# Block 1's attention in a one-core transformer kernel: from probabilities stationary, token rows out, to values stationary in two column halves, feature rows out

## The reference, cut to what matters

```python
s = einsum('bqkgd,bskd->bkgqs', q, k) * ATTN_SCALE
p = softmax(s, axis=-1)
a = einsum('bkgqs,bskd->bqkgd', p, v)
...
mix = concatenate([rmsnorm(a, attn_out_norm), rmsnorm(sc, conv_out_norm)], axis=-1)
x = x + m[:, :, 5] * (mix @ w_mix_out)
```

## Time and profile before

| | us |
|---|---|
| median of 3 runs | 1551.4 (1549.38 to 1552.7) |
| the profiled execution, its own time | 1551.04 |
| its span in the profile | 1548.8 |
| PE busy | 1414.5 (91%) |
| DVE busy | 1071.8 (69%) |
| ACT busy | 598.5 (39%) |
| attention stage (first scores to first `out` c matmul) | 439.7 to 501.6 |

### The profile page before, as it was taken

The page is one execution under the profiler, slowest core; times in us unless marked ns, Lnnn a source line. Parts: engine busy times, 40 slices in busy tenths (PEclk is TensorE's granted clock), DMA queues, the critical chain, the costliest instruction groups (busy, mean ns, idle before and its releaser), DMA issues.

```text
span 1548.8 us, 20067 instructions
## 1 busy us (share of the span) xinstructions
PE 1414.5 (91%) x7471; PEld 1053.9 (68%) x7471; DVE 1071.8 (69%) x2243; ACT 598.5 (39%) x1349; POOL 383.4 (25%) x377
## 2 busy tenths in 40 slices
PE   8999999999999999999999988999988777778777
PEld 6788888889887999999899955665433323223222
DVE  4787775547876687777896476757798666666454
ACT  4422122224556544445565233423343333333222
POOL 0100110002100100011006134445555444445330
PEclk7999999999999999999999999999999999999999
DMA  8864685446641465555545699999999999999997
GB/s 332 294 219 129 202 290 175 140 138 184 214 139 54 128 206 184 171 172 182 153 148 190 229 383 414 419 421 421 421 421 421 421 422 421 421 421 421 422 421 293
DMA packets 86479, 435.96 MB, mean 281 GB/s; under 512 B 9520, under 2 KB 13616, under 8 KB 53616
## 3 DMA queue, kind: packets, MB, share of 16 engines
q0 software_dynamic: 45024, 298.08, 48.2%
q1 hardware_dynamic: 41360, 136.62, 27.1%
HBM read 433.61 MB, written 1.05 MB: 281 GB/s over the span
## 4 chain that ended last, share of the span: by engine, by line
PE 61%; DMA 21%; DVE 13%; ACT 3%; issue 1%; POOL 0%; SPq 0%; ACTq 0%; POOLq 0%
PE ps L623 14%; PE ps L625 14%; PE ps L624 14%; DMA ring<-in_puv,AB 13%; PE ps L1064 10%; DMA HF<-in_puv,AB 7%; PE ps L984 5%; DVE WR L1454 2%; DVE ring L2242 1%; ACT WR L1084 1%; PE ps L663 1%; DMA ring<-in_f1i 1%; DVE HF L2242 1%; PE ps L1003 0%; DVE AF L2242 0%
## 5 line engine op out<-in xcount | busy, mean ns | idle before, releaser
L623 PE MATMUL ps<-HR,WR 128*128 128x512 f32 (+2 forms) x1064 | 344.8, 324 | 3.3 <-DVE WR L1454 1.4
L625 PE MATMUL ps<-HR,WR 128*128 128x512 f32 (+2 forms) x1064 | 339.7, 319 | 0.0
L624 PE MATMUL ps<-HR,WR 128*128 128x512 f32 (+2 forms) x1064 | 339.6, 319 | 0.0
L1454 DVE TENSOR_TENSOR WR<-ring,WR 128x1024 fp32r<-128x1024 f32 (+1 forms) x217 | 252.8, 1172 | 114.6 <-ACT WR L1084 114.4
L1084 ACT CAST WR<-ring 128x1024 fp32r<-128x1024 f32 (+1 forms) x217 | 212.6, 986 | 277.1 <-PE ps L625 273.5
L623 PEld LDWEIGHTS ps<-HR,WR 128*128 128x128 f32 x1064 | 202.7, 191 | 20.3 <-issue 2.4
L625 PEld LDWEIGHTS ps<-HR,WR 128*128 128x128 f32 x1064 | 202.6, 190 | 13.9
L624 PEld LDWEIGHTS ps<-HR,WR 128*128 128x128 f32 x1064 | 202.8, 191 | 13.7 <-issue 0.2
L1064 PE MATMUL ps<-AF,AB 128*128 128x512 f32 x264 | 126.9, 604 | 34.5 <-ACT AB L1439 34.5
L1429 ACT ACTIVATE AB<-AB 128x2 f32<-128x2 f32 x129 | 26.2, 203 | 322.0 <-DVE AB L2242 321.9
L623 PE MATMUL ps<-AR,WR 128*128 128x256 f32 (+1 forms) x471 | 147.4, 313 | 2.4 <-DVE AF L1835 2.4
(11 more groups left out here) (339 smaller groups left out, 2340.6 us busy)
## 6 DMA issues: line engine op xcount, KB each, us to landing
AB<-in_w_adaT POOLq DMA_DIRECT2D x56, 512.0 KB, 4.8
ring<-in_f1i SPq DMA_DIRECT2D x44, 512.0 KB, 4.8
ring<-in_f2i SPq DMA_DIRECT2D x44, 512.0 KB, 3.7
ring<-in_w SPq DMA_DIRECT2D x29, 512.0 KB, 3.7
ring<-in_f1o SPq DMA_DIRECT2D x21, 512.0 KB, 4.2
ring<-in_w_ada SPq DMA_DIRECT2D x16, 512.0 KB, 7.6
ring<-in_f2o SPq DMA_DIRECT2D x16, 512.0 KB, 3.7
ring<-in_mi SPq DMA_DIRECT2D x12, 512.0 KB, 4.5
```

Source lines behind the costliest of these rows:

```text
L623: e.matmul(o, l[0], r[0], start=first, stop=False)
L624: e.matmul(o, l[0], r[1], start=False, stop=False)
L625: return e.matmul(o, l[1], r[0], start=False, stop=last)
L1454: e.tensor_tensor(WS[:, m % NSP, 1, 0:nk * cols], ring[:, ring_of(m) % NS, 0:nk * cols], WS[:, m % NSP, 0, 0:nk * cols].bitcast(F32), ALU. ...
```

## The change

The product with the values is turned round. `pv` is now a step for two heads, one of each key/value head: the values (128 keys by 64 features) are stationary and the transposed exponentials move, 128 columns. The even head's result goes to partitions 0 to 63 and column half 0 of the array, the odd head's to partitions 64 to 127 and column half 1. The output has features on the partitions, so it needs no transpose, but the softmax sums and the norm, which were one number per partition, now are one number per column:

- `an` i 0: DVE takes the reciprocal of the sums, ACT copies it over 64 columns each into `aN` (128x512), PE transposes that ("over", 4 transposes). p 1: ACT copies it from PSUM to `R(2, 4)`.
- p 2: DVE multiplies `o` with it. p 3: ACT squares. p 4: PE sums the squares over partitions with ones (4 matmuls, line 831), DVE makes the reciprocal, 128x128. p 5 (`roots` for tile 0): ACT root, 128x128, and DVE applies root and gain in four instructions of 128 columns. p 6: ACT and DVE make high and low part from SBUF.
- The gain comes as four columns of the constants, so one broadcast DMA (`aon`) goes.

```diff
+    norms[8] = [("an", 0, 0)]
+    norms[9].append(("an", 0, 1))
-             12: [("an", 0, 0)], 13: [("an", 0, 1)], 15: [("roots",)], 16: [("cn", 2, 0)], 17: [("cn", 2, 1), ("cn", 2, 2)],
-             18: [("cn", 2, 3)], 19: [("cn", 2, 4), ("an", 0, 2)]}
+             12: [("an", 0, 2), ("an", 0, 3)], 13: [("an", 0, 4)], 15: [("roots",)], 16: [("cn", 2, 0), ("an", 1, 0)],
+             17: [("cn", 2, 1), ("cn", 2, 2), ("an", 1, 1)], 18: [("cn", 2, 3)], 19: [("cn", 2, 4), ("an", 0, 5)]}
-        if n >= 4:
-            out.append(("pv", n - 4))
+        if n >= 4 and n % 2:
+            out.append(("pv", (n - 5) // 2))
-    out += [("an", 1, 0), ("an", 1, 1), ("an", 1, 2), ("out", "c", 0), ("an", 0, 3), ("out", "c", 1), ("an", 1, 3),
-            ("out", "c", 2), ("out", "c", 3)]
+    out += [("an", 1, 2), ("an", 1, 3), ("out", "c", 0), ("an", 0, 6), ("an", 1, 4), ("out", "c", 1), ("an", 1, 5),
+            ("out", "c", 2), ("an", 1, 6), ("out", "c", 3)]
...
                     for k in range(4):
-                        x = e.matmul(o, PT[:, s[1] % 4, k, :], kvN[:, k, 128 + 64 * (hd % 2):192 + 64 * (hd % 2)],
-                                     start=k == 0, stop=k == 3)
-                    x.then_inc(*mm.to("pv", s[1]))
+                        for g in range(2):
+                            x = e.matmul(o[64 * g:64 * g + 64, :], kvN[:, k, 128 + 64 * g:192 + 64 * g],
+                                         PT[:, (2 * s[1] + g) % 4, k, :], start=k == 0, stop=k == 3)
+                            if k == 3:
+                                x.then_inc(*mm.to("pv", 2 * s[1] + g))
...
+                elif s[0] == "an" and s[2] == 4:
+                    o = bank("rms", "a", s[1])[:, 0:128]
+                    q.wait_ge(*ac.at("sq", "a", s[1]))
+                    for j in range(4):
+                        x = e.matmul(o, K("ones"), R(2, 4)[:, 128 * j:128 * j + 128], start=j == 0, stop=j == 3)
...
+                    if p == 0:
+                        q.wait_ge(*dv.at("over sums", i))
+                        e.copy(aN[:, i, :].rearrange("p (h d) -> p h d", h=8),
+                               hs[:, 104 + 8 * i:112 + 8 * i].unsqueeze(2).broadcast_to([128, 8, 64])).then_inc(
+                                   *ac.to("spread sums", i))
+                    elif p == 1:
+                        evac(R(2, 4), ("over", i), bank_of("over", i)[:, :])
...
+                    elif p == 4:
+                        recip(("a", i), ra_[:, i, :], 128, 1.0 / 512)
...
-                    e.dma_start(aon, T["aon"].partition_broadcast(128)).then_inc(s_aon, 16)
```

More of the change, by code:

```diff
@@ L399, in program @@
         cq, sq_, ck_, sk_ = (AB[:, 2048 + 128 * n:2176 + 128 * n].rearrange("p (i d) -> p i d", i=2) for n in range(4))
-        aon = AB[:, 2560:3072]
+        ra_ = AB[:, 2560:2816].rearrange("p (i q) -> p i q", i=2)
         gqk = K("gqk").rearrange("p (n d) -> p n d", n=4)
@@ L814, in tensor_program @@
                 elif s[0] == "an" and s[2] == 0:
[L815 to L818, removed]
+                    o = bank("over", s[1])
+                    q.wait_ge(*ac.at("spread sums", s[1]))
                     for j in range(4):
                         x = e.transpose(o[:, 128 * j:128 * j + 128], aN[:, s[1], 128 * j:128 * j + 128], K("ident"))
-                    x.then_inc(*mm.to("turn", "a", s[1]))
+                    x.then_inc(*mm.to("over", s[1]))
+                elif s[0] == "an" and s[2] == 2:
+                    banks.held.discard(banks.of["o", s[1]])
+                elif s[0] == "an" and s[2] == 4:
[3 more added lines that the diff above has]
+                        x = e.matmul(o, K("ones"), R(2, 4)[:, 128 * j:128 * j + 128], start=j == 0, stop=j == 3)
+                    x.then_inc(*mm.to("rms", "a", s[1]))
                 elif s[0] == "out":
@@ L1241, in scalar_program @@
                     root(("c",), R(0, 1))
-                    root(("a", 0), hs[:, 122:123])
+                    root(("a", 0), ra_[:, 0, :])
                 elif s[0] == "cn" and s[1] == 2 and s[2] < 4:
@@ L1246, in scalar_program @@
                     e.copy(MX[k][0], F[:, k % 3, 0:256]).then_inc(*ac.to("mx hi", k))
[L1247 to L1258, removed]
+                elif s[0] == "an":
+                    _, i, p = s
+                    if p == 0:
[5 more added lines that the diff above has]
+                        evac(R(2, 4), ("over", i), bank_of("over", i)[:, :])
+                    elif p == 3:
+                        q.wait_ge(*dv.at("ps", "o", i))
+                        e.activation(R(2, 4), aN[:, i, :], ACT.Square).then_inc(*ac.to("sq", "a", i))
+                    elif p == 5 and i:
+                        root(("a", 1), ra_[:, 1, :])
+                    elif p == 6:
+                        q.wait_ge(*dv.at("an", i))
+                        e.copy(MXR[:, 0, 4:8, 128 * i:128 * i + 128], aN[:, i, :].rearrange("p (j q) -> p j q", j=4)).then_inc(
+                            *ac.to("mxa hi", i))
                 elif s[0] == "out":
@@ L1828, in vector_program @@
                     _, i, p = s
-                    ri, ra_ = hs[:, 104 + 8 * i:112 + 8 * i], hs[:, 122 + i:123 + i]
                     if p == 0:
                         q.wait_ge(*ac.at("ps", "s", 8 * i + 7))
-                        e.reciprocal(ri, hs[:, 88 + 8 * i:96 + 8 * i]).then_inc(*dv.to("rsum", i))
-                        q.wait_ge(*dv.now())
+                        e.reciprocal(hs[:, 104 + 8 * i:112 + 8 * i], hs[:, 88 + 8 * i:96 + 8 * i]).then_inc(*dv.to("over sums", i))
+                    elif p == 2:
@@ L1834, in vector_program @@
                         q.wait_ge(*mm.at("pv", 8 * i + 7))
[L1835 to L1844, removed]
-                        q.wait_ge(*ac.at("root", "a", i))
[L1846 to L1849, removed]
+                        q.wait_ge(*ac.at("over", i))
@@ new lines, in vector_program @@
+                        e.tensor_tensor(aN[:, i, :], bank_of("o", i)[:, :], R(2, 4), ALU.mult).then_inc(*dv.to("ps", "o", i))
+                    elif p == 4:
+                        recip(("a", i), ra_[:, i, :], 128, 1.0 / 512)
+                    elif p == 5:
+                        q.wait_ge(*ac.at("root", "a", i))
+                        for j in range(4):
+                            a = aN[:, i, 128 * j:128 * j + 128]
+                            e.scalar_tensor_tensor(out=a, in0=a, scalar=C("aon")[:, j:j + 1], in1=ra_[:, i, :], op0=ALU.mult,
+                                                   op1=ALU.mult).then_inc(*dv.to("an", i))
+                    elif p == 6:
@@ L1850, in vector_program @@
                         hi, low = (MXR[:, n, 4:8, 128 * i:128 * i + 128] for n in range(2))
                         q.wait_ge(*ac.at("mxa hi", i))
-                        e.tensor_tensor(low, bank_of("turn", "a", i)[:, :].rearrange("p (j q) -> p j q", j=4),
-                                        hi.bitcast(F32), ALU.subtract).then_inc(*dv.to("ps", "turn", "a", i))
-                        dv.also("mxa", i)
+                        e.tensor_tensor(low, aN[:, i, :].rearrange("p (j q) -> p j q", j=4), hi.bitcast(F32),
+                                        ALU.subtract).then_inc(*dv.to("mxa", i))
@@ L2507, in layout @@
         "conv": cw, "con": cols(i["conv_out_norm"][0]),
+        "aon": cols(i["attn_out_norm"][0][heads]),
         "kvn": cols(i["kv_norm_g_2"][0]), "qn2": cols(i["q_norm_g_2"][0]), "kn2": cols(i["k_norm_g_2"][0]),
@@ L2520, in layout @@
         "miq": wide(mi[:, heads], 512), "mikv": wide(mi[:, 512:768], 256), "mi": tiles(mi[:, 768:]),
-        "moc": pairs(mo[512:]), "moa": pairs(mo[:512][heads]), "aon": i["attn_out_norm"][0][heads],
+        "moc": pairs(mo[512:]), "moa": pairs(mo[:512][heads]),
         "f2i": tiles(i["w_ffn2_in"][0]), "f2o": tiles(i["w_ffn2_out"][0]),
```

13 lines of the change are left out of this document (7 added, 6 removed).

## The result

Before 1552.37 us (median of 17 runs, 1549.38 to 1560.67), after 1557.46 (17 runs, 1553.49 to 1562.1). Ratio 1.0033, 95% interval 1.0024 to 1.0042: slower by 0.33%, some 5.1 us. The forecast was 1555.5 and slower.

The account below looks back on a forecast made before the run. PE, busy 91% of the span, was taken to pass its time on nearly one for one. Walk terms -1.0 + 2.65 - 0.6 + 3.0 - 1.35 + 0.2 = +2.9, clock +1.4, total +4.3: 1555.5 us, range 1552.3 to 1559.

Parts of the forecast that it names:

- The walk: Attention stage followed in after's order with before's durations, between pairs of `front`, through the `out` tiles: +2.9 us without clock.
- the clock: Falls to 1.2 GHz behind PE waits: one of two new waits costs 1.5, the old fall keeps its price: +1.4 us.
- the pair: Two heads' `pv` product on column halves takes 1.15 us instead of 1.64, saving 0.5.
- Rival (b): A `pv` pair costs less, 0.82 us (total 1553.7) or 0.5 (1551.9), so not slower; chance 0.12.
- Rival (c): The column halves do not overlap: pair 2.1 us, +5.7 more, total 1561.2; chance 0.08.
- the first and third wait: PE idles ahead of "over": 2.85 us for tile 0, behind DVE's late reciprocal, and some 4.6 for tile 1.
- No wait before the first `out`: Before's 2.43 us PE wait for the bank of `o` goes, as `out` has another bank.
- the second wait: PE idles 2.75 us before the sum over partitions (line 831), ahead of `front` 14, waiting for ACT's square.
- the sentence that no PSUM bank handed out again is still in use: Said of the part up to `front` 8: no reused bank makes PE wait; that part changes by -1.0 us.
- Rival (a): The clock stays up behind both new waits: +2.9 us, 1554.4, just inside no change; chance 0.22.

Follow-up runs that it names:

- x1: After with throwaway matmuls filling PE's three long waits: 1552.24 us, ratio to before 1.0000.
- x7: Before with five throwaway matmuls filling PE's 2.43 us wait ahead of the first output tile: 1549.46 us, ratio to before 0.9980.
- x4: After with tile 0's reciprocal and copy of sums ahead of the last filler's weight, PE's transposes behind the third pair: 1553.22 us, ratio to before 1.0009.
- x2: After with the bank of `o` of tile 0 given back one step later, so `back` 11 takes another: 1557.28 us, ratio to before 1.0027.
- x3: After with a pair's two column halves one after the other instead of alternating: 1559.4 us, ratio to before 1.0044.
- x10: After with five throwaway matmuls in the first of the three long waits only: 1555.03 us, ratio to before 1.0020.
- x8: Before with the bank of `o` of tile 1 held until the first output tile has another: 1547.18 us, ratio to before 0.9964.
- x5: After reordered: x4 and x2 together, tile 0's sum of squares and tile 1's copy and transposes also moved: 1545.84 us, ratio to before 0.9954.
- x9: x5 with a pair's two column halves one after the other instead of alternating: 1547.48 us, ratio to before 0.9967.

## Why the prediction was right, and where it was off

**Right: slower, by waits.** x1 runs after's order at full clock, x7 before's. Their stretches are 91.25 and 88.21, difference 3.04; by the ratios 3.1. The walk's sum without the clock was +2.9. Part of this closeness is luck: behind `front` 12 the walk is 0.4 too low for one part and 0.3 too high for the next.

| part | walk | x1 | after |
|---|---|---|---|
| to `front` 8, against before | -1.0 | -1.16 | -1.16 |
| `front` 8 to 10 | 9.35 | 9.29 | 11.11 |
| `front` 10 to 12 | 4.1 | 4.17 | 5.19 |
| `front` 12 to 14 | 6.8 | 7.21 | 9.47 |
| `front` 14 to the first `out` | 11.3 | 10.98 | 12.82 |

**Right: the pair.** 1.02 us and 0.1 for the entry, 1.12 for the forecast 1.15. Rival (b), 0.82, is out. The Trainium skill, page TensorEngine Tiling (Array Packing), section Theoretical Speedup, puts the gain for a dimension of 64 or less at up to 2x; here 1.64 to 1.12 is 1.46x. Rival (c) is out; its 2.1 was wrong as a bound too, since the halves in turn cost 1.51. Why a 128-column matmul beside another half is cheaper than `total`'s column is open.

**Right: the first and third wait.** 2.74 for 2.85 and 4.22 for 4.6, with the releasers named, the reciprocal behind the weight's low part (478.97 behind 477.83). x4 undid exactly that. No wait before the first `out`.

**Wrong place: the second wait.** The prediction had it before 831, released by 1269, with `back` 11 and the pair ahead of it. It stood at `back` 11, released by DVE's product (1852), which ends at 492.70 + 0.69 = 493.39; `back` 11 starts at 493.44. The step that failed is the sentence that no PSUM bank handed out again is still in use. I made it for the part up to `front` 8, where it holds, and did not ask again after `("an", 0, 2)`, where `Banks.take` gives `back` 11 the bank that this same step is emptying. Size 2.80 for 2.75, but `back` 11 and the pair moved behind it: 7.21 in x1 for 6.8. x2 put the wait where I had it, at 2.64, and the part took 6.91.

**Mis-sized: the clock.** The term was +1.4, for one new fall of two possible, with the old one taken over at its 1.5. It was a choice, not a reading. After had three falls in the profiled execution, and without them it is 5.2 us faster (x1). Before without its fall is 3.1 us faster (x7), though only 1.5 of it shows in the profiled execution. So by the times the clock adds 5.2 - 3.1 = 2.1 to the difference and the waits the other 3.1. That the two make up the measured 5.1 to 5.2 is no check, since the same four kernels give both; and each ratio's interval is 1.3 to 1.6 us either way, so the times alone can't tell 2.1 from 1.4. By the stretches of the profiled executions the clock adds (97.84 - 91.25) - (89.71 - 88.21) = 5.09 and the waits 3.04. What is shown is three falls where the forecast had two, and waits of some 3 us by both rulers; the clock's share in an average execution lies somewhere about 2 and stays rough. That the total came so near, 5.1 for 4.3, owes something to luck.

The miss in absolute time is 1557.5 for 1555.5. Half of it is the median of before, 1552.4 over 17 runs for 1551.4 over 3, 0.8 is the difference (5.1 for 4.3), and 0.2 is the prediction's own sum: 1551.4 and 4.3 make 1555.7.

Rival (a), no fall behind the new waits, is out for the profiled execution by its stretches of 0.50 and 0.54. x3 and x10 show that a fall can stay away behind a wait of that length; how often it does in after was not counted.

**What the turned product is worth.** Before with the bank alone (x8) 0.9964, the turned product with all steps in place (x5) 0.9954: stretches 85.65 and 84.33. So beside a kernel without the old wait the swap is worth 1.3 us by the profile, which the times are too coarse to confirm, while the placing of its steps makes 1557.46 - 1545.84 = 11.6 us between after and x5 (12.3 by the ratios). x9 says the same: its pair, 1.51 us, costs nearly the old product's 1.64, and its ratio is still 0.9967.

## What to carry to other kernels

When a division or a norm moves to another axis, its helper steps (reciprocal, spread, transpose, sum) come to stand on three engines. Walk each engine's queue to the place where the matrix engine would need the result, and put the matrix engine's share one step behind that; also ask for each PSUM bank handed out from then on who has yet to empty it. A wait of 2 to 4 us ahead of dense work costs time and can cost some 1.7 us more in clock (5.2 us for three in x1), in the old kernel too (3.1 us for one in x7): look for such waits before asking what a faster matmul gives.

## What the runs showed of the hardware

- In this stage of the profiled executions the clock fell to 1.2 GHz during or right behind PE waits of 2.43 (before), 2.64 and 3.15 (x2), 2.74, 2.80 and 4.22 (after), 2.79 and 3.82 (x3), 3.11 and 4.30 (x4) and 4.30 us (x10), and did not at others of 2.74 (x3) and 2.79 (x10). At waits up to 1.36 (x5) it did not. The length alone doesn't decide; what does was not tried.
- Matmuls whose results are thrown away kept the clock up in x1: three waits with 0.49, 0.63 and 0.85 us left idle, and 1.00 throughout the stage.
- Two heads' 16 trace instructions take 1.02 us on column halves in alternation, 1.51 in turn, and 1.64 on the whole array with 64 columns moving.
